# Attention's probabilities turned in 32x32 blocks and moved by ScalarE's DMA queue, in a two-block layer stack

## The chip, the cores and the metric

One core of one Trainium2 chip. The metric is the device time of one execution in microseconds, of which three were taken. The profile is of one execution of its own.

## The reference

Two stacks of two layers each, on 256 tokens of width 2048, in float32. The first (a hybrid of windowed attention, spatial gating and gated linear attention) is the same before and after. The change lies in the second:

```python
h = x @ w_in                       # q, k, v, z for 12 heads "a" and 12 heads "b", 128 wide; forget and gate logits
qa, ka = rope(qa), rope(ka)
out_a = dilated_mixture(qa, ka, va)              # causal softmax attention, banded patterns
out_b = softmax(qb @ kb.T * 128**-0.5 + cum[t] - cum[s], causal) @ vb
up_a, up_b = (out_a * silu(za)) @ w_up_a, (out_b * silu(zb)) @ w_up_b
y = (g_a * up_a + g_b * up_b) @ w_out
x = layer_norm(alpha * x + y)
```

The kernel computes out_a as one softmax over all 256 keys, with the logarithm of how often a key occurs in the patterns added to its score (mask_a).

## The kernel before, in words

**Stream of granules.** The weights of a layer come as granules of 256 rows by 512 columns (512 KB), into a ring of four slots (`raw`). SyncE loads them (L310) when VectorE has done with a slot. ScalarE copies a granule to `whi` rounded to the float32r format (`hi`, L372) once TensorE has given back the slot that is four granules older. VectorE subtracts to get the rest, `wlo` (`lo`, L489). TensorE multiplies high by high, low by high and high by low: twelve matmuls of 512 columns a granule (`accumulate`, L860), of which the last four wait for `wlo`. Eight granules are one chunk of 512 output columns. The plan of chunks (`second_plan`) is q, k, v, z for each group of four heads, three groups, then four gate chunks, four up-projections, the same once more for heads "b", then four output chunks. There are six groups a layer and two layers, so twelve groups in all.

**Attention is written into this stream by hand.** For each group r counts granules from the start of its q chunk (`group_step`), and each engine does its part of the attention at fixed r, behind its work on the granule (ScalarE, VectorE) or ahead of it (TensorE: `fills2` into the two banks psT, `units2` into the two banks psS). Since ScalarE and VectorE work ahead of TensorE, step r is not the same moment on all engines.

- r = 12 to 14 and 20 to 22: q and k are rotated (VectorE, heads "a") or copied (ScalarE, heads "b") into `stage`. Then VectorE turns 32x32 blocks (L615) from `stage` into `blocks`, and POOL issues 16 DMAs (L325), which move each quarter of the partitions to each quarter of the columns. This makes qT and kT, features on partitions. A DMA moves 32 partitions with eight pieces of 128 bytes.
- r = 26, 27, 28: score units s0 (four heads, tokens 0 to 127), s1 and s2 (two heads each, tokens 128 to 255, 256 keys), L829. An f32 matmul is two passes, each with a weight load of its own.
- r = 30, 31, 32: VectorE adds the mask or bias and takes the row maxima (L642 to L648). r = 31, 32, 33: ScalarE takes the exponentials with their row sums (L416); at r = 31 it also copies v out.
- r = 31, 32, 33 on TensorE: the 128x128 probabilities are transposed against an identity, four per unit (L812, into psT). r = 35, 36, 37: ScalarE copies them to `probT` (L392).
- r = 36, 37: output units o0 and o1 (L839), with `probT` as the stationary operand and v moving.
- r = 38: ScalarE evacuates z with Silu (L429). r = 39: reciprocals. r = 40, 41: VectorE scales and multiplies by z (L664, L668). r = 42: VectorE turns the blocks of the product into `zb` (L674), and POOL issues 16 DMAs to zT, which shares memory with `probT`. r = 50: ScalarE and VectorE split zT into `ahi` and `alo` for the up-projection (L437, L731).

POOL issues its DMAs in the order q, k, z of each group (`regrouped`), with the gate rows between. SyncE's queue has only the weights and the result.

In the first block, L2147 on VectorE multiplies `zt` in place by a transposed operand, both read as pieces of m elements with a gap of m elements, for m = 128, 64, 32, 16, 8, 4, 2 and 1:

```python
a = zt[:, i % 2, :].rearrange("p (n s m) -> p n s m", s=2, m=m)[:, :, half, :]
last = dve.tensor_tensor(a, a, b, ALU.mult)
```

## Time and profile before

| | |
|---|---|
| runs (median, lowest to highest of 3) | 2801.91 us, 2800.36 to 2802.63 us |
| profiled execution, its own time | 2799.75 us |
| its span, first to last instruction | 2798.0 us |
| mean granted TensorE clock | 0.994 of full speed |
| instructions | 35964 |
| DMA | 622.74 MB, 223 GB/s |

The profile lists the work of each engine, PE for TensorE's matmuls and PEld for its weight loads, DVE for VectorE, ACT for ScalarE, POOL for GpSimd and SPq for SyncE's DMA issues. L860 is line 860 of the kernel. Durations of single matmuls overlap, so that of a stretch is read from the starts. The first block takes the first 839 us or so; the second the rest.

### The profile page before, as it was taken

The page shows a single profiled execution, that of the slowest core. Times are in us where ns is not written, and L with a number is a line of the kernel's source. Part 1 is how long each engine was busy: PE and PEld are TensorE (multiplying, and loading weights), DVE is VectorE, ACT ScalarE, POOL GpSimd, SP SyncE. Part 2 cuts the span into 40 slices and gives each one's busy share as a digit, 9 for nine tenths or more (in the row PEclk, how much of TensorE's full clock was granted, in tenths as well). Part 3 has the DMA queues.
Part 4 walks back from the last instruction along what each step waited for, and adds up shares of the span by engine and source line. Part 5 has one row for each costly group of instructions (what it writes and reads, how often), then busy time and mean ns, then how long its engine had stood idle before and what let it go on. Part 6 is the DMA issues. An engine that isn't in the chain of part 4 may idle for free.

```text
span 2798.0 us, 35964 instructions
## 1 busy us (share of the span) xinstructions
PE 2757.6 (99%) x13157; PEld 2253.2 (81%) x13157; DVE 1817.0 (65%) x2220; ACT 1346.3 (48%) x1765; POOL 370.9 (13%) x653
## 2 busy tenths in 40 slices
PE   8899999999999999999999999999999999999998
PEld 5477887888888888888888888888888888888886
DVE  7889899778657556655555556575565545555565
ACT  3255646556544453544444544444445444445443
POOL 0000010000001223100133100022131011331000
PEclk9999999999999999999999999999999999999999
DMA  9987798865655566566566566565566665665554
GB/s 397 414 311 241 272 342 307 309 222 190 215 194 181 188 201 205 185 220 196 191 202 203 191 196 223 181 195 187 191 203 205 208 199 183 206 206 187 193 213 148
DMA packets 178617, 622.74 MB, mean 223 GB/s; under 512 B 27688, under 2 KB 27984, under 8 KB 173088
## 3 DMA queue, kind: packets, MB, share of 16 engines
q1 hardware_dynamic: 155376, 583.08, 60.3%
q0 software_dynamic: 23088, 37.56, 4.6%
q8 instruction: 104, 1.70, 0.3%
q14 instruction: 49, 0.40, 0.0%
HBM read 599.51 MB, written 2.14 MB: 215 GB/s over the span
## 4 chain that ended last, share of the span: by engine, by line
PE 90%; DMA 4%; DVE 4%; ACT 1%; issue 0%; SPq 0%; DVEq 0%; ACTq 0%
PE acc L860 65%; PE acc L2455 16%; DMA raw<-in_w 2%; DVE wlo L1865 1%; PE psS L839 1%; PE psS L829 1%; DMA scr<-in_w_early 1%; PE psS L2455 1%; PE psS L2421 1%; PE psT L812 1%; PE psT L2378 1%; DMA mraw<-in_w_early 1%; DVE raw L1900 0%; PE psS L2440 0%; PE psT L2340 0%
## 5 line engine op out<-in xcount | busy, mean ns | idle before, releaser
L489 DVE TENSOR_TENSOR wlo<-raw,whi 128x1024 fp32r<-128x1024 f32 x670 | 819.4, 1224 | 783.7 <-ACT whi L372 782.0
L372 ACT ACTIVATE whi<-raw 128x1024 fp32r<-128x1024 f32 x670 | 708.9, 1059 | 980.3 <-PE acc L860 964.4
L860 PE MATMUL acc<-whi,tokens_hi 128*128 128x512 f32 x2304 | 632.3, 395 | 0.5 <-DVE tokens_lo L303 0.3
L860 PE MATMUL acc<-whi,tokens_lo 128*128 128x512 f32 x2304 | 618.2, 389 | 0.0
L860 PE MATMUL acc<-wlo,tokens_hi 128*128 128x512 f32 x2304 | 618.1, 389 | 0.0
L860 PEld LDWEIGHTS acc<-whi,tokens_lo 128*128 128x128 f32 x2304 | 432.4, 188 | 91.5
L860 PEld LDWEIGHTS acc<-wlo,tokens_hi 128*128 128x128 f32 x2304 | 432.4, 188 | 91.0
L860 PEld LDWEIGHTS acc<-whi,tokens_hi 128*128 128x128 f32 x2304 | 425.7, 188 | 85.6 <-DVE tokens_lo L303 0.9
L1564 ACT ACTIVATE whi<-raw 128x1024 fp32r<-128x1024 f32 x160 | 168.7, 1058 | 200.8 <-PE acc L2455 116.2
L1865 DVE TENSOR_TENSOR wlo<-raw,whi 128x1024 fp32r<-128x1024 f32 x160 | 195.3, 1223 | 82.2 <-ACT whi L1564 81.3
L2455 PE MATMUL acc<-whi,tokens_hi 128*128 128x512 f32 x800 | 226.1, 403 | 1.9 <-DVE tokens_lo L1974 1.2
L2455 PE MATMUL acc<-wlo,tokens_hi 128*128 128x512 f32 x800 | 215.6, 390 | 0.7 <-DVE wlo L1865 0.7
L2455 PE MATMUL acc<-whi,tokens_lo 128*128 128x512 f32 x800 | 215.6, 390 | 0.0
L325 POOL DMA_DIRECT2D probT<-prob x192 | 110.3, 583 | 619.4 <-DVE prob L674 619.4
L2455 PEld LDWEIGHTS acc<-wlo,tokens_hi 128*128 128x128 f32 x800 | 150.0, 188 | 33.3 <-DVE wlo L1865 1.4
L2455 PEld LDWEIGHTS acc<-whi,tokens_lo 128*128 128x128 f32 x800 | 150.2, 188 | 32.8
L2455 PEld LDWEIGHTS acc<-whi,tokens_hi 128*128 128x128 f32 x800 | 143.0, 188 | 35.3 <-issue 3.5
L325 POOL DMA_DIRECT2D qT<-blocks x192 | 110.5, 584 | 448.6 <-DVE blocks L615 447.6
L325 POOL DMA_DIRECT2D kT<-blocks x192 | 110.2, 583 | 149.3 <-DVE blocks L615 149.3
L860 PE MATMUL acc<-whi,ahi 128*128 128x512 f32 x384 | 103.2, 391 | 0.0
L1564 ACT ACTIVATE whi<-mraw 128x1024 fp32r<-128x1024 f32 x64 | 67.7, 1058 | 73.2 <-PE acc L2455 59.7
L860 PE MATMUL acc<-wlo,ahi 128*128 128x512 f32 x384 | 102.7, 389 | 0.0
(355 smaller groups left out, 2434.2 us busy)
## 6 DMA issues: line engine op xcount, KB each, us to landing
raw<-in_w SPq DMA_DIRECT2D x838, 512.0 KB, 4.2
raw<-in_w_late SPq DMA_DIRECT2D x80, 512.0 KB, 5.0
mraw<-in_w SPq DMA_DIRECT2D x64, 512.0 KB, 4.7
mraw<-in_w_late SPq DMA_DIRECT2D x48, 512.0 KB, 4.8
y<-in_w_early SPq DMA_DIRECT2D x12, 1024.0 KB, 15.4
mraw<-in_w_early SPq DMA_DIRECT2D x7, 1024.0 KB, 14.9
scr<-in_w_early SPq DMA_DIRECT2D x7, 1024.0 KB, 14.8
sgl<-in_w_early SPq DMA_DIRECT2D x6, 1024.0 KB, 15.0
```

What stands on the lines that cost most here:

```text
L325: pool.dma_start(dst[c * QUAD:(c + 1) * QUAD, :, b * QUAD:(b + 1) * QUAD], src[b * QUAD:(b + 1) * QUAD, :, c * QUAD:(c + 1) * QUAD]).then_ ...
L372: act.activation(whi[:, n % SLOTS, :], raw[:, n % SLOTS, :], ACT.Copy).then_inc(s_hi, 1)
L489: dve.tensor_tensor(wlo[:, n % SLOTS, :], raw[:, n % SLOTS, :], whi[:, n % SLOTS, :].bitcast(F32), ALU.subtract).then_inc(s_lo, 1)
L812: t = pe.transpose(bank[:, k * P:(k + 1) * P], prob[:, name[2], k * P:(k + 1) * P], ident[:])
L829: m = pe.matmul(out, qT[:, h, tb * P:(tb + 1) * P], kT[:, h, 0:w], start=True, stop=True)
L839: m = pe.matmul(bank[:, h * HD:(h + 1) * HD], probT[:, u, col * P:(col + 1) * P], v[:, s, h * HD:(h + 1) * HD], start=(s == 0), stop=(s == ...
L860: m = pe.matmul(acc[c % 2][:, tb, :], a[:, kk, tb * P:(tb + 1) * P], b[:, n % SLOTS, k * CW:(k + 1) * CW], start=(kk == 0 and q == 0), sto ...
L1564: act.activation(whi[:, n % SLOTS, :], slot(("w", n)), ACT.Copy).then_inc(s_hi, 1)
L1865: dve.tensor_tensor(wlo[:, n % SLOTS, :], slot(("w", n)), whi[:, n % SLOTS, :].bitcast(F32), ALU.subtract).then_inc(s_lo, 1)
L2378: t = pe.transpose(bank[:, k * SEQ + tb * P:k * SEQ + (tb + 1) * P], src[:, tb, cols[k]:cols[k] + P], ident[:])
L2421: m = pe.matmul(out[:, k * P:(k + 1) * P], key[rows, kcol:kcol + P], query[rows, qcol:qcol + P], start=True, stop=True)
L2455: m = pe.matmul(bank_a(gc)[:, tb, :], a[:, kt, tb * P:(tb + 1) * P], b[:, n % SLOTS, k * CW:(k + 1) * CW], start=(g == 0 and k == 0 and q ...
```

## The change

- **Probabilities.** TensorE's twelve identity transposes a group and ScalarE's three copies go. At r = 33 (R_PROB) VectorE waits for all exponentials and turns the blocks of all 1536 columns in one instruction, into `pb`, which lies over qT and half of kT (now one tile `qkT`). At r = 34 ScalarE waits for that, and for the previous group's `alo`, and issues 16 DMAs on its own queue to `pT` (all of `probT`). Each moves 32 partitions with one piece of 1536 bytes.
- **Long pieces.** VectorE writes turned blocks so that what one DMA moves lies together: q, k and z go in one piece of 1 KB a partition. For this q and the probabilities are laid out `by_column` (a token's 8, or 12, values side by side), k and z `by_quad` (runs of 32). TensorE reads qT with a step of 8 elements and pT with a step of 12 as stationary operands, and kT as moving operand in runs of 32. z is kept in the order of heads (`zheads`).
- **Order.** All three score units stand at r = 26, s2 in a psT bank. Both output units stand at r = 37. VectorE takes the scores at r = 29 to 31, ScalarE the exponentials at r = 30 to 32. VectorE's outputs move to r = 41 and 42, z's blocks to 43. `s_blk` counts four per group instead of three. POOL's q and k moves wait for the previous group's probabilities (`s_pT`) instead of its scores, and its z move no longer waits for `alo`.

The other lines of the diff only renumber waits (3 to 4 per group, `16 * QUADS * QUADS` to `MOVED`).

```diff
--- before.py
+++ after.py
@@ -83,10 +83,12 @@

 R_Q, R_K = 14, 22
 R_SCORES = 26
-R_BLOCKS = R_SCORES + 16
+R_PROB = R_SCORES + 7
+R_BLOCKS = R_SCORES + 17
 R_SPLIT = 50
 QUAD = 32
 QUADS = P // QUAD
+MOVED = 16 * QUADS * QUADS
...
@@ -109,8 +111,8 @@
     if c == 0:
         out += [("x", 0), ("x", 1)] if g == 0 else [("x", g + 1)] if g < KT // 2 - 1 else []
     for grp, r in group_step(c, g):
-        if 0 <= r - R_SCORES - 5 <= 2:
-            out += [("p", grp, r - R_SCORES - 5)]
+        if r == R_SCORES:
+            out += [("s", grp, 2)]
     if c and CHUNKS2[c - 1][0] == "u" and CHUNKS2[c - 1][1] >= NCW and g == 3:
         j = CHUNKS2[c - 1][1] - NCW
...
@@ -121,10 +123,10 @@

     out = []
     for grp, r in group_step(c, g):
-        if 0 <= r - R_SCORES <= 2:
-            out += [("s", grp, r - R_SCORES)]
-        if 0 <= r - R_SCORES - 10 <= 1:
-            out += [("o", grp, r - R_SCORES - 10)]
+        if r == R_SCORES:
+            out += [("s", grp, 0), ("s", grp, 1)]
+        if r == R_SCORES + 11:
+            out += [("o", grp, 0), ("o", grp, 1)]
...
     alo = sb("alo", [P, KT_UP, SEQ], F32R)
     gb = sb("gb", [P, TB, D])
     stage = sb("stage", [P, TB, CW])
-    qT = sb("qT", [P, HPG, SEQ])
-    kT = sb("kT", [P, HPG, SEQ])
+    qkT = sb("qkT", [P, 2 * HPG, SEQ])
+    qT, kT = qkT[:, 0:HPG, :], qkT[:, HPG:, :]
     v = sb("v", [P, TB, CW])
     z = sb("z", [P, TB, CW])
     prob = sb("prob", [P, 3, CW])
     probT = sb("probT", [P, 3, CW])
-    zb = prob[:, 0:TB, :].rearrange("p b (k t) -> p (b k) t", t=HD)
-    zT = probT[:, 0:TB, :].rearrange("p b (k t) -> p (b k) t", t=HD)
+    pT = probT[:].rearrange("p u n -> p (u n)")
+    pb = qkT[:].rearrange("p h t -> p (h t)")[:, 0:3 * CW]
+    zb = prob[:, 0:TB, :].rearrange("p b t -> p (b t)")
+    zT = probT[:, 0:TB, :].rearrange("p b t -> p (b t)")
     blocks = sb("blocks", [P, TB, CW])
     rtmp = blocks[:, 1, :]
-    heads = stage[:].rearrange("p b n -> p (b n)").rearrange("p (h b e) -> p b h e", b=TB, e=HD)
+    heads, zheads = (t[:].rearrange("p b n -> p (b n)").rearrange("p (h b e) -> p b h e", b=TB, e=HD)
+                     for t in (stage, z))
     mask_a = sb("mask_a", [P, P + SEQ])
...
         return psT[FILL2[name] % 2]

+    def by_feature(tile):
+
+        return tile.rearrange("p (k c j) -> p k c j", c=QUADS, j=QUAD)
+
+    def by_quad(tile):
+
+        return tile.rearrange("p (c k j) -> p k c j", c=QUADS, j=QUAD)
+
+    def by_column(tile):
+
+        return tile.rearrange("p (c j k) -> p k c j", c=QUADS, j=QUAD)
+
     def attended_views(grp):

         k = HPG * (grp % 3)
-        return [t[:, k:k + HPG, :].rearrange("p k (b t) -> p b k t", b=TB) for t in (ahi, alo)] + [
-            zT.rearrange("p (b k) t -> p b k t", b=TB)]
+        return [by_feature(t[:, k:k + HPG, :].rearrange("p k t -> p (k t)")) for t in (ahi, alo)] + [by_quad(zT)]
...

+    def blocks_moved(queue, dst, src, signal):
+
+        dst, src = (t.rearrange("p (c n) -> p c n", c=QUADS) for t in (dst, src))
+        for b in range(QUADS):
+            for c in range(QUADS):
+                queue.dma_start(dst[c * QUAD:(c + 1) * QUAD, b, :], src[b * QUAD:(b + 1) * QUAD, c, :])\
+                    .then_inc(signal, 16)
+
     def gpsimd(pool):
         pool.wait_ge(s_ym, NCW * DEPTH)
         for tile, name in ((mask_a, "mask_a"), (mask_b, "mask_b"), (tables, "tables")):
             pool.dma_start(tile[:], dram[name]).then_inc(s_const, 16)
-        def blocks_moved(dst, src, signal):
-
-            for b in range(QUADS):
-                for c in range(QUADS):
-                    pool.dma_start(dst[c * QUAD:(c + 1) * QUAD, :, b * QUAD:(b + 1) * QUAD],
-                                   src[b * QUAD:(b + 1) * QUAD, :, c * QUAD:(c + 1) * QUAD]).then_inc(signal, 16)
-
         def regrouped(l, grp):

             n = NGRP * l + grp
             for i, (dst, signal) in enumerate(((qT, s_qT), (kT, s_kT))):
-                pool.wait_ge(s_blk, 3 * n + i + 1)
-                if grp:
-                    pool.wait_ge(*unit_full(l, ("s", grp - 1, 2)))
-                elif l:
-                    pool.wait_ge(*unit_full(l - 1, ("s", NGRP - 1, 2)))
-                blocks_moved(dst[:].rearrange("p h (b t) -> p (h b) t", b=TB),
-                             blocks[:].rearrange("p b (k t) -> p (b k) t", t=HD), signal)
-            pool.wait_ge(s_blk, 3 * n + 3)
-            if n:
-                pool.wait_ge(s_alo, n)
-            blocks_moved(zT, zb, s_zT)
+                pool.wait_ge(s_blk, 4 * n + i + 1)
+                if n:
+                    pool.wait_ge(s_pT, MOVED * n)
+                blocks_moved(pool, dst.rearrange("p h t -> p (h t)"), blocks[:].rearrange("p b t -> p (b t)"), signal)
+            pool.wait_ge(s_blk, 4 * n + 4)
+            blocks_moved(pool, zT, zb, s_zT)
...
-            def fill_copy(name, dst):
-                act.wait_ge(*filled(l, name))
-                act.activation(dst, bank_t(name)[:], ACT.Copy).then_inc(s_tfree[FILL2[name] % 2], 1)
-
             def evacuate(c, dst, func, scale=1.0):
                 act.wait_ge(*multiplied(l, c))
                 src = acc[c % 2][:]
-                if dst is heads:
+                if dst is not v:
                     src = src.rearrange("p b (h e) -> p b h e", e=HD)
...
@@ -418,18 +427,19 @@
                     p.then_inc(s_exp, 1)
                 if r == 31:
                     evacuate(c0 + 2, v, ACT.Copy)
-                if 0 <= r - R_SCORES - 9 <= 2:
-                    u = r - R_SCORES - 9
-                    if u == 0 and NGRP * l + grp:
-                        act.wait_ge(s_alo, NGRP * l + grp)
-                    fill_copy(("p", grp, u), probT[:, u, :])
+                if r == R_PROB + 1:
+                    n = NGRP * l + grp
+                    act.wait_ge(s_blk, 4 * n + 3)
+                    if n:
+                        act.wait_ge(s_alo, n)
+                    blocks_moved(act, pT, pb, s_pT)
                 if r == R_SCORES + 12:
                     if NGRP * l + grp:
-                        act.wait_ge(s_blk, 3 * (NGRP * l + grp))
-                    evacuate(c0 + 3, z, ACT.Silu)
+                        act.wait_ge(s_blk, 4 * (NGRP * l + grp))
+                    evacuate(c0 + 3, zheads, ACT.Silu)
...
                     dve.wait_ge(*acc_read(l, group_chunk(grp) + which))
                 if which:
-                    dve.wait_ge(s_qT, 16 * QUADS * QUADS * (NGRP * l + grp + 1))
-                dve.transpose(blocks[:].rearrange("p b n -> p (b n)"), stage[:].rearrange("p b n -> p (b n)"))\
+                    dve.wait_ge(s_qT, MOVED * (NGRP * l + grp + 1))
+                dve.transpose((by_column, by_quad)[which](blocks[:].rearrange("p b n -> p (b n)")),
+                              by_feature(stage[:].rearrange("p b n -> p (b n)")))\
                     .then_inc(s_blk, 1)

...
-                if 0 <= r - R_SCORES - 4 <= 2:
-
-                    u = r - R_SCORES - 4
+                if 0 <= r - R_SCORES - 3 <= 2:
+
+                    u = r - R_SCORES - 3
                     name = ("s", grp, u)
-                    bank = UNIT2[name] % 2
+                    if u < 2:
+                        bank, full, free = psS[UNIT2[name] % 2], unit_full(l, name), s_sfree[UNIT2[name] % 2]
+                        read = unit_read(l, name)
+                    else:
+                        bank, full, free = bank_t(name), filled(l, name), s_tfree[FILL2[name] % 2]
+                        read = copied(l, name)
...
-                    dve.wait_ge(*unit_full(l, name))
+                    dve.wait_ge(*full)
...
-                    dve.tensor_tensor(p, psS[bank][:].rearrange("p (h s) -> p h s", s=w), m, ALU.add)\
-                        .then_inc(s_sfree[bank], 1)
-                    dve.wait_ge(*unit_read(l, name))
+                    dve.tensor_tensor(p, bank[:].rearrange("p (h s) -> p h s", s=w), m, ALU.add).then_inc(free, 1)
+                    dve.wait_ge(*read)
...
+                if r == R_PROB:
+                    dve.wait_ge(s_exp, at(l, 3 * NGRP, 3 * grp + 3))
+                    dve.transpose(by_column(pb), by_feature(prob[:].rearrange("p u n -> p (u n)"))).then_inc(s_blk, 1)
...
-                if 0 <= r - R_SCORES - 14 <= 1:
-
-                    tb = r - R_SCORES - 14
+                if 0 <= r - R_SCORES - 15 <= 1:
+
+                    tb = r - R_SCORES - 15
                     name = ("o", grp, tb)
                     bank = UNIT2[name] % 2
                     dve.wait_ge(*unit_full(l, name))
...
-                    dve.tensor_tensor(z[:, tb, :], z[:, tb, :], rtmp, ALU.mult).then_inc(s_att, 1)
+                    dve.tensor_tensor(zheads[:, tb], zheads[:, tb], t, ALU.mult).then_inc(s_att, 1)
                 if r == R_BLOCKS:
                     n = NGRP * l + grp
                     dve.wait_ge(s_att, TB * (n + 1))
-                    if n:
-                        dve.wait_ge(s_zT, 16 * QUADS * QUADS * n)
-                    dve.transpose(zb.rearrange("p a t -> p (a t)"), z[:].rearrange("p b n -> p (b n)")).then_inc(s_blk, 1)
+                    dve.wait_ge(s_blk, 4 * n + 3)
+                    dve.transpose(by_quad(zb), by_feature(z[:].rearrange("p b n -> p (b n)"))).then_inc(s_blk, 1)

...
+            def turned_heads(tile):
+
+                return tile.rearrange("p h t -> p (h t)").rearrange("p (c h t j) -> p h t c j", c=QUADS, h=HPG, t=TB)
+
+            def queries(tile):
+
+                return tile.rearrange("p h t -> p (h t)").rearrange("p (t h b) -> p h b t", h=HPG, b=TB)
+
+            def scores(name, bank):
+
+                _, grp, u = name
+                pe.wait_ge(s_qT, MOVED * (NGRP * l + grp + 1))
+                pe.wait_ge(s_kT, MOVED * (NGRP * l + grp + 1))
+                w, tb = (P, 0) if u == 0 else (SEQ, 1)
+                for b in range(CW // w):
+                    h = b + max(0, 2 * (u - 1))
+                    m = pe.matmul(bank[:, b * w:(b + 1) * w].rearrange("p (t c j) -> p t c j", c=QUADS, j=QUAD),
+                                  queries(qT)[:, h, tb], turned_heads(kT)[:, h, 0:tb + 1], start=True, stop=True)
+                return m
...
                 else:
-
-                    pe.wait_ge(s_exp, at(l, 3 * NGRP, 3 * name[1] + name[2] + 1))
-                    for k in range(4):
-                        t = pe.transpose(bank[:, k * P:(k + 1) * P], prob[:, name[2], k * P:(k + 1) * P], ident[:])
+                    t = scores(name, bank)
...
                 if name[0] == "s":
-                    _, grp, u = name
-                    if u == 0:
-                        pe.wait_ge(s_qT, 16 * QUADS * QUADS * (NGRP * l + grp + 1))
-                        pe.wait_ge(s_kT, 16 * QUADS * QUADS * (NGRP * l + grp + 1))
-                    w, tb = (P, 0) if u == 0 else (SEQ, 1)
-                    for b in range(CW // w):
-                        h = b + max(0, 2 * (u - 1))
-                        out = bank[:, b * w:(b + 1) * w]
-                        m = pe.matmul(out, qT[:, h, tb * P:(tb + 1) * P], kT[:, h, 0:w], start=True, stop=True)
+                    m = scores(name, bank)
...
                     _, grp, tb = name
                     if tb == 0:
                         pe.wait_ge(*acc_read(l, group_chunk(grp) + 2))
-                    for p in ((0,), (1, 2))[tb]:
-                        pe.wait_ge(*copied(l, ("p", grp, p)))
+                        pe.wait_ge(s_pT, MOVED * (NGRP * l + grp + 1))
                     for h in range(HPG):
                         for s in range(tb + 1):
                             u, col = (0, h) if tb == 0 else (1 + h // 2, 2 * (h % 2) + s)
-                            m = pe.matmul(bank[:, h * HD:(h + 1) * HD], probT[:, u, col * P:(col + 1) * P],
+                            m = pe.matmul(bank[:, h * HD:(h + 1) * HD], pT.rearrange("p (t k) -> p k t", k=3 * HPG)[:, HPG * u + col],
                                           v[:, s, h * HD:(h + 1) * HD], start=(s == 0), stop=(s == tb))
```

## Rows read from the trace of the kernel before

**Rows 1.** The page, first part: span, busy time, share and instructions

```profile
span 2798.0 us, 35964 instructions
...
PE 2757.6 (99%) x13157; PEld 2253.2 (81%) x13157; DVE 1817.0 (65%) x2220; ACT 1346.3 (48%) x1765; POOL 370.9 (13%) x653
```

**Rows 2.** Waits of PE, 850 to 2780 us: total, times, longest

```profile
PE psT L802 <- DVE x L525: 0.9, 1, 0.9
PE acc L860 <- DVE tokens_lo L495: 0.2, 1, 0.2
```

**Rows 3.** Waits of all engines, whole span: total us, times, longest

```profile
ACT whi L372 <- PE acc L860: 964.4, 577, 5.5
DVE wlo L489 <- ACT whi L372: 782.0, 582, 4.4
...
ACT whi L372 <- DMA raw<-in_w: 15.8, 9, 4.6
```

**Rows 4.** Chain that ended last, 900 to 1030 us: start, us, what

```profile
921.88 0.89 PE psS L829 x8
922.78 2.74 PE acc L860 x12
925.51 0.86 PE psS L829 x4
...
930.01 8.21 PE acc L860 x36
938.22 0.44 PE psT L812 x4
938.66 2.77 PE acc L860 x12
...
945.07 8.21 PE acc L860 x36
953.28 0.89 PE psS L839 x8
...
956.90 1.78 PE psS L839 x16
958.69 57.14 PE acc L860 x252
```

**Rows 5.** Groups by shape, PE, from 640 us: busy us, mean ns

```profile
L812 PE MATMUL psT<-ident,prob 128*128 128x128 f32 x144 | 21.5, 271 | 0.0
```

**Rows 6.** Timeline of ACT, 920 to 985 us: start, us, instruction, idle before

```profile
921.98 1.06 ACT L372 ACTIVATE whi<-raw 128x1024 fp32r<-128x1024 f32 x1 [1.66 <-PE acc L860]
...
930.32 1.28 ACT L416 ACT_TABLE_LOAD   x1
...
942.50 0.58 ACT L392 ACTIVATE probT<-psT 128x512 f32<-128x512 f32 x1
```

**Rows 7.** Timeline of DVE, 918 to 985 us

```profile
926.70 1.23 DVE L489 TENSOR_TENSOR wlo<-raw,whi 128x1024 fp32r<-128x1024 f32 x1 [2.40 <-ACT whi L372]
...
966.48 1.24 DVE L674 STREAM_TRANSPOSE prob<-z 128x1024 f32<-128x1024 f32 x1
```

**Rows 8.** Line L2147, DVE: ns min/median/max, first and last start

```profile
L2147 DVE TENSOR_TENSOR zt<-zt,gain x32: 415/417/420, 191.2 to 669.2; 128x256 f32<-128x256 f32 x32
```

**Rows 9.** SyncE's issues: line L310, and the timeline, 28.0 to 29.2 us

```profile
L310 SPq DMA_DIRECT2D raw<-in_w x668: 332/333/353, 839.2 to 2766.3; - x167
...
28.10 0.33 SPq L1461 DMA_DIRECT2D y<-in_w_early  x1
28.47 0.43 SPq L1467 DMA_DIRECT2D b_kT<-in_w  x1
```

**Rows 10.** POOL's issues: timeline 907 to 925 us, and line L325

```profile
907.64 9.18 POOL L325 DMA_DIRECT2D kT<-blocks  x16 [12.17 <-DVE blocks L615]
...
L325 POOL DMA_DIRECT2D kT<-blocks x192: 582/582/593, 907.6 to 2512.7; - x192
...
DMA to landing us min/median/max: 1.8/3.0/5.4
```

More of the change, by code:

```diff
@@ L216, in second_block @@
     s_kT = sem("c_kT")
+    s_pT = sem("c_pT")
     s_zT = sem("c_zT")
@@ L403, in attention @@
                 if grp >= 3 and r == R_Q - 2:
-                    act.wait_ge(s_blk, 3 * (NGRP * l + grp) - 1)
+                    act.wait_ge(s_blk, 4 * (NGRP * l + grp) - 2)
                     evacuate(c0, heads, ACT.Copy, SCALE2)
                 if grp >= 3 and r == R_K - 2:
-                    act.wait_ge(s_blk, 3 * (NGRP * l + grp) + 1)
+                    act.wait_ge(s_blk, 4 * (NGRP * l + grp) + 1)
                     evacuate(c0 + 1, heads, ACT.Copy)
-                if 0 <= r - R_SCORES - 5 <= 2:
-                    u = r - R_SCORES - 5
+                if 0 <= r - R_SCORES - 4 <= 2:
+                    u = r - R_SCORES - 4
                     act.wait_ge(s_max, at(l, 3 * NGRP, 3 * grp + u + 1))
@@ L420, in attention @@
                     evacuate(c0 + 2, v, ACT.Copy)
[L421 to L425 removed]
+                if r == R_PROB + 1:
[4 more added lines that the diff above has]
+                    blocks_moved(act, pT, pb, s_pT)
                 if r == R_SCORES + 12:
                     if NGRP * l + grp:
[L428 to L429 removed]
+                        act.wait_ge(s_blk, 4 * (NGRP * l + grp))
+                    evacuate(c0 + 3, zheads, ACT.Silu)
                 if r == R_SPLIT:
                     hi_view, _, src = attended_views(grp)
[L432 removed]
+                    act.wait_ge(s_zT, MOVED * (NGRP * l + grp + 1))
                     if grp >= 3:
@@ L582, in rope @@
                     if which:
-                        dve.wait_ge(s_blk, 3 * n + 1)
-                        dve.wait_ge(s_qT, 16 * QUADS * QUADS * (n + 1))
+                        dve.wait_ge(s_blk, 4 * n + 1)
+                        dve.wait_ge(s_qT, MOVED * (n + 1))
                     elif n:
-                        dve.wait_ge(s_blk, 3 * n - 1)
+                        dve.wait_ge(s_blk, 4 * n - 2)
                 half = HD // 2
@@ L637, in attention @@
                             dve.wait_ge(s_cmask, l + 1)
-                    dve.wait_ge(*unit_full(l, name))
+                    dve.wait_ge(*full)
                     if u == 0 and NGRP * l + grp:
-                        dve.wait_ge(s_zT, 16 * QUADS * QUADS * (NGRP * l + grp))
+                        dve.wait_ge(s_zT, MOVED * (NGRP * l + grp))
                     p = prob[:, u, :].rearrange("p (h s) -> p h s", s=w)
-                    dve.tensor_tensor(p, psS[bank][:].rearrange("p (h s) -> p h s", s=w), m, ALU.add)\
-                        .then_inc(s_sfree[bank], 1)
-                    dve.wait_ge(*unit_read(l, name))
+                    dve.tensor_tensor(p, bank[:].rearrange("p (h s) -> p h s", s=w), m, ALU.add).then_inc(free, 1)
+                    dve.wait_ge(*read)
                     if grp >= 3 and u == 0:
@@ L659, in attention @@
                         dve.wait_ge(*acc_read(l, c0 + 3))
-                        dve.wait_ge(s_kT, 16 * QUADS * QUADS * (NGRP * l + grp + 1))
+                        dve.wait_ge(s_kT, MOVED * (NGRP * l + grp + 1))
                     else:
```

1 line of the change is left out of this document (removed).

## The prediction

> **What bounds the kernel now.** Four views, in this order. The page's first part: TensorE is busy for 99% of the span, VectorE and ScalarE for 65% and 48% [rows 1]. A busy share of pipelined matmuls could still hide waiting, so next the waits, asked over the second block: TensorE has two, together 1.1 us, both at a layer's start [rows 2], while ScalarE waits 964 us for TensorE (it splits a granule as soon as TensorE has given a ring slot back) and VectorE 782 us for ScalarE [rows 3]. So in the second block the time is that of TensorE's own queue. Third, the chain of waits around one group of heads, which in this stretch is TensorE alone [rows 4]. Outside attention 252 matmuls take 57.14 us: 0.2268 us each, 2.72 us a granule of twelve. The attention work stands between the granules as extra pieces. A second group, a layer later, has the same pieces within 0.01 us, so one group is read and taken twelve times (2 layers of 6). Fourth, the timelines of ScalarE and VectorE around that group [rows 6, 7], because the change hands work to both, and an engine that is not the bound becomes it once a granule comes late.
>
> **Removed from TensorE.** 144 transposes [rows 5], twelve a group, in three pieces of 0.44 us, and a granule beside such a piece is drawn at 2.76 to 2.77 or (three of them) 8.21 instead of 2.72 and 8.16: 3 x 0.44 + 3 x 0.05 = 1.47 us a group [rows 4]. Twelve groups: 17.6 us. Nothing else hides this work, so all of it is on the path.
>
> **Merged on TensorE.** The three score units now stand together, and so do the two output units. Each break between kinds of matmul costs some 0.02 to 0.05 us (0.89, 0.86, 0.86 and granules of 2.74, 2.77 and 8.21 in place of 2.72 and 8.16). Two breaks of scores and one of outputs go: about 0.1 us a group, 1.2 us in all.
>
> **The operands' layout, the open price.** The number of attention matmuls and columns stays. But the stationary operand of the scores (queries) is now read with 8 elements, 32 bytes, from one column to the next, and that of the outputs (probabilities) with 12, 48 bytes; before both were contiguous. The keys, which move, come in runs of 32 elements. No row shows TensorE reading a spread operand. The lower bound is nothing: the nearest row of any spread read is VectorE's multiplication in the first block, whose pieces shrink from 128 elements to one with a gap as long, and all 32 of them take 415 to 420 ns [rows 8]. It reaches only a step of 8 bytes, on another engine. The upper bound: a load that takes two steps a column. A pass of 128 columns has a pitch of 0.89/8 = 0.111 us, where load and pass are about equally long, and a pass of 256 columns 0.86/4 = 0.215 us [rows 4] (an f32 product is two passes, so s0 has 8, each later score unit 4, the outputs 8 and 16). If a spread load lasts as long as the 256-column pass, the 8 + 24 short passes rise from 0.111 to 0.215: 3.3 us a group, 40 us in all; the 256-column ones cover it. A gain from the layout is excluded: passes and columns are the same. I take nothing, since the one measured row says so, and keep 40 us for the range and for a rival.
> The Trainium skill speaks against the change here: "Advanced Engine Details and Errata", section "SBUF Cachelines", says memory is read in lines of 16 bytes, needs at least two hits on a line to hide the access, and pays when every access is in another line. Eight or twelve f32 elements apart is another line each time. The multiplication of [rows 8], with two elements a line, doesn't contradict it. By it the sum would end near the upper bound, at 2821, which is the result of the first rival.
>
> **ScalarE.** Three copies of 0.58 us a group go; it waits for TensorE there [rows 3, 6], so they are worth nothing. What it gains: 16 DMA issues at granule step 34 with two waits in front, on the previous group's low half (done at step 18, long past) and on VectorE's turned blocks. No row shows ScalarE issuing a DMA. Bounds: SyncE's issues take 0.33 us, one straight behind another 0.43 us, starts 0.37 us apart [rows 9]; POOL's take 0.58 us [rows 10], which is descriptor work of another kind. Nearest is SyncE's: I take 0.40, 6.4 us for the sixteen, with 5.3 and 9.3 us as ends. Queued behind them is the split of granule 35, for which TensorE waits. Let T be TensorE's start of granule 31, when slot and step 34 of ScalarE come free (each split starts as a granule ends: 921.98 with the first score at 921.88 [rows 4, 6]). The split of 34 lasts until T+1.1 (1.06 us). VectorE at step 33: the previous splits end at about T-1.1 by ScalarE's timeline moved one step forward [rows 6] (split, table load 1.28, four exponentials, v's evacuation, two more pairs), its subtraction costs 1.14 from start to start, so the new transpose runs from T+0.1. It is 1536 elements wide against 1024 at 1.24 us [rows 7]: 1.86 us, until T+1.95. ScalarE idles 0.85 us there. Issues until T+8.35, split of 35 until T+9.4. TensorE starts granule 35 at T + 4 x 2.72 = T+10.9. Slack 1.5 us, and afterwards ScalarE catches up, 1.06 us against 2.72. The point from which TensorE waits is an issue of 0.49 us. Cost taken: nothing, covered by the four-slot ring.
>
> **VectorE.** 12 transposes of 1.86 us, 22 us in all, and the same additions and maxima one step earlier. In the second block it mostly waits for ScalarE [rows 3]; granule 33 costs it 1.2 + 1.9 us against 2.72, and its lead over TensorE is several us (it subtracts granule 30 at 926.70 [rows 7]; TensorE comes to it after 935, two granules of 2.72 behind 930.01 [rows 4]). Nothing. If the blocks' spread output slowed it to double, only ScalarE's wait would grow, by 1.9 us.
>
> **POOL and the moves.** POOL issues as many DMAs as before (192 three times, 0.58 us each), with pieces of 1 KB where there were eight of 128 bytes. Keys: last issue at 916.8, landing 3.0 us (up to 5.4) after an issue, scores at 921.88 [rows 4, 10]: same distance as before, about 2 us. The turned z comes one granule later (step 43), is issued over 9.2 us and is wanted at step 50, 19 us on; the next queries may wait about 1 us behind it and have the 22 us until the keys. The probabilities' transfers are 16 x 48 KB, at most 6.4 + 4 us after T+1.95, and the outputs stand at granule 37, T+16.3: covered by 4 us. SyncE's loads share the DMA engines, but ScalarE waited only 15.8 us on them in all [rows 3], and the slot of 35 freed 5 us late still leaves its next load landed before TensorE needs it.
>
> **Sum.** Profiled execution: 2799.75 us (span 2798.0, 1.75 outside) [rows 1]. 2799.75 - 17.6 - 1.2 = 2781.0. The median of the runs is 2801.9, 2.2 above the profiled one, so I forecast 2782. About 0.2%, 5.6 us, is what a measurement here can tell from no change.
>
> **Rivals.**
> 1. *Spread weight loads become the bound* (chance 0.36, slower). Place: the eight passes of s0 and the 24 of the outputs. Price +40 us, so 2821 to 2823. It decides against the change from 0.16 us a load instead of 0.111: 18.8/(12 x 32) = 0.05 us more cancels the gain. For: these passes have load and pass equally long, so nothing hides a longer load. Against: the even 415 to 420 ns of [rows 8].
> 2. *ScalarE's issues hold up the split of granule 35* (0.10). At POOL's 0.58 us the issues end at T+11.2, the split at T+12.3: 1.4 us waiting a group, 17 us; result 2782 to 2799, and still below before unless VectorE's transpose is slow as well (another 1.9 us a group, 22 us).
> 3. *Both* (0.10): 2828 to 2862.
> 4. *A load dearer by about half the bound* (0.06): 2797 to 2807, no change.
> That the change doesn't do what it says, that is, the transposes leave TensorE and nothing falls, would need a wait that TensorE doesn't have before [rows 2]; it is in rivals 2 and 3.
>
> **Numbers.** The forecast's own case has 0.38, 2778 to 2785. Faster by over 0.2% (below 2796.3): 0.38 and most of rival 2, 0.46. Within: part of rivals 2 and 4, 0.10. Slower: rivals 1 and 3 and the rest, 0.44. The range goes from 2778 up over rival 1 with a little waiting, to 2829; most of rival 3 is left out.
>
> **What the profile will show.** No identity transposes of probabilities; TensorE's chain with one piece of scores of 16 passes and one of outputs of 24. Right: those take 2.6 and 2.7 us, so 5.3 together. Rival 1: outputs near 5.1 us and s0 near 1.7, weight loads of these lines longer than 188 ns or with gaps of 0.2 us. Rival 2: waits of TensorE on ScalarE's whi, twelve times, near granule 35. ScalarE's issues at 0.33 to 0.43 us would confirm the slack; the wide transpose at 1.86 us VectorE's term. The forecast is wrong if any pass of 128 columns has a pitch above 0.16 us or if TensorE waits over 1.5 us a group.

## The result and the profile after

The changed kernel takes 2915.6 us (median of 4 runs, 2911.1 to 2916.7), against 2801.5 for the kernel before: a ratio of 1.0405 (95% interval 1.0393 to 1.0418), 114 us slower. The prediction was 2782, with 2829 as the upper end.

The page's first part, to be held against [rows 1]:

```profile
span 2913.1 us, 35810 instructions
...
PE 2822.9 (97%) x13013; PEld 2315.8 (79%) x13013; DVE 1858.4 (64%) x2232; ACT 1324.8 (45%) x1729; POOL 321.3 (11%) x653
```

The 144 transposes are gone, yet TensorE is busy for 65 us more, and its span has grown by 115: there is slower work and there is idle time. The waits of TensorE, 850 to 2900 us, name the idle time; before there were only waits of the last two kinds, 1.1 us in all ([rows 2]):

```profile
PE acc L885 <- ACT whi L385: 48.7, 12, 4.9
PE psT L839 <- DVE x L535: 1.1, 2, 0.9
PE acc L885 <- DVE tokens_lo L505: 0.2, 1, 0.2
```

Twelve waits, one a group, for ScalarE's split of a granule. The chain of waits of the first group says what stands behind it (start, us, what; compare [rows 4]):

```profile
921.00 0.94 PE psT L816 x4
921.95 2.87 PE psS L816 x12
924.82 2.78 PE acc L885 x12
...
938.78 2.92 DVE qkT L666
941.71 0.60 ACTq L339
...
952.36 1.06 ACT whi L385
...
953.47 7.36 PE acc L885 x24
960.83 6.30 PE psS L864 x24
967.12 57.17 PE acc L885 x252
```

VectorE's wide transpose ends at 941.7, ScalarE's queue then issues sixteen transfers until 952.3, the next split comes at 952.36, and TensorE starts granule 35 at 953.47. ScalarE's timeline shows the burst as one line:

```profile
941.71 10.54 ACTq L339 DMA_DIRECT2D probT<-qkT  x16
952.36 3.90 ACT L385 ACTIVATE whi<-raw 128x1024 fp32r<-128x1024 f32 x4 [12.74 <-issue]
```

Two more things are in the chain. The scores take 0.94 + 2.87 = 3.81 us, the outputs 6.30, where before they took 2.61 and 2.67. And the two granules behind the wait take 7.36 us where 5.44 are due. The table by stretches (us, PE, PEld, DVE, ACT, POOL busy, then the granted TensorE clock, DMA share, GB/s) shows why:

```profile
942.00:948.30 6.30, 6.30 (x30) 5.21 (x29) 0.73 (x1) 0.00 (x0) 0.00 (x0) 1.00 0.51 147
949.00:953.47 4.47, 0.34 (x3) 0.01 (x1) 0.03 (x1) 1.11 (x2) 0.00 (x0) 1.00 0.29 77
953.47:957.92 4.45, 4.45 (x12) 3.49 (x13) 4.45 (x4) 4.42 (x5) 0.00 (x0) 0.62 0.39 131
957.92:960.66 2.74, 2.74 (x13) 2.30 (x12) 1.25 (x2) 1.62 (x2) 0.00 (x0) 1.00 0.97 298
```

After the idle stretch the granted clock is 0.62 of full speed on average, a mixture of the levels 1.2 and 2.4 GHz, and the twelve matmuls of that granule take 4.45 us for 2.72. One granule later it is full again. Not every group is like the first. In the second the wait is 4.9 us, and the granule behind it looks like this:

```profile
1057.50:1062.79 5.29, 5.29 (x12) 4.13 (x13) 4.62 (x4) 5.10 (x5) 0.00 (x0) 0.50 0.54 153
```

It takes 5.29 us, all of it at the lower level. Summed over the twelve groups (from the starts of the matmuls), the two granules behind the wait take 90.8 us where 65.3 are due: 26 us more, and not twelve times the first group's 1.7. The single lines (ns min/median/max) show the slow loads, and VectorE's writing:

```profile
L864 PEld LDWEIGHTS psS<-v,probT x288: 342/369/373, 960.4 to 2670.6; 128*128 128x128 f32 x144
L816 PEld LDWEIGHTS psS<-qkT x144: 335/336/338, 921.6 to 2628.6; 128*128 128x128 f32 x144
...
L625 DVE STREAM_TRANSPOSE blocks<-stage x24: 1239/1686/2169, 883.7 to 2608.7; 128x1024 f32<-128x1024 f32 x24
L666 DVE STREAM_TRANSPOSE qkT<-prob x12: 2972/2977/2989, 938.7 to 2643.1; 128x1536 f32<-128x1536 f32 x12
...
L339 ACTq DMA_DIRECT2D probT<-qkT x192: 514/612/1382, 941.7 to 2656.0; - x192
L339 POOL DMA_DIRECT2D probT<-prob x192: 496/496/546, 979.2 to 2692.9; - x192
```

**Theory A**, as it stood before the experiments: three losses per group. The spread operands cost (3.81 - 2.61) + (6.30 - 2.67) = 4.8 us, the wait 4.1, the low clock behind it 1.7. Twelve times: 58 + 49 + 21 = 128 us, less the 18.8 that the prediction counted as gain, is 109 of the 114. The 21 are the first group's 1.7 us taken twelve times; with the 26 us of all twelve in their place the sum is 114. The rivals, one against each term: the wait comes from VectorE and not from the queue (B); the passes are slow by the moving keys or by contention with the transfers (D, E); the clock is low for another reason (M).

### The profile page after: what moved, and what is told of

Its sections match the earlier page's. It is cut to its first block, busy times and chain, and to the rows that moved or that the text cites. A ratio compares the mean times of both kernels' runs of the same rounds, so it can differ in the third digit from the quotient of the medians.

```text
span 2913.1 us, 35810 instructions
## 1 busy us (share of the span) xinstructions
PE 2822.9 (97%) x13013; PEld 2315.8 (79%) x13013; DVE 1858.4 (64%) x2232; ACT 1324.8 (45%) x1729; POOL 321.3 (11%) x653
## 4 chain that ended last, share of the span: by engine, by line
PE 79%; DVE 6%; ACT 5%; DMA 4%; ACTq 4%; issue 1%; SPq 0%; DVEq 0%
PE acc L885 55%; PE acc L2480 15%; ACTq L339 4%; DMA raw<-in_w 3%; PE psS L864 3%; ACT whi L385 2%; ACT prob L425 1%; DVE wlo L1890 1%; DVE qkT L666 1%; PE psS L816 1%; DMA scr<-in_w_early 1%; PE psS L2480 1%; PE psS L2446 1%; DMA mraw<-in_w_early 1%; ACT L425 1%
## 5 line engine op out<-in xcount | busy, mean ns | idle before, releaser
L885 PE MATMUL acc<-whi,tokens_hi 128*128 128x512 f32 x2304 | 635.1, 397 | 49.3 <-ACT whi L385 48.7
L885 PE MATMUL acc<-whi,tokens_lo 128*128 128x512 f32 x2304 | 627.3, 394 | 0.0
L885 PEld LDWEIGHTS acc<-whi,tokens_hi 128*128 128x128 f32 x2304 | 435.3, 191 | 144.4 <-ACT whi L385 53.8
L885 PEld LDWEIGHTS acc<-whi,tokens_lo 128*128 128x128 f32 x2304 | 439.2, 191 | 93.5
L339 POOL DMA_DIRECT2D qkT<-blocks x384 | 187.7, 497 | 606.0 <-DVE blocks L625 603.0
L2480 PE MATMUL acc<-whi,tokens_lo 128*128 128x512 f32 x800 | 215.6, 390 | 0.0
L339 POOL DMA_DIRECT2D probT<-prob x192 | 93.9, 497 | 791.8 <-DVE prob L691 520.3
L2480 PEld LDWEIGHTS acc<-whi,tokens_lo 128*128 128x128 f32 x800 | 150.2, 188 | 32.8
L2480 PEld LDWEIGHTS acc<-whi,tokens_hi 128*128 128x128 f32 x800 | 143.0, 188 | 35.3 <-issue 3.7
L885 PE MATMUL acc<-whi,alo 128*128 128x512 f32 x384 | 102.6, 389 | 0.0
```

The source lines that it names most:

```text
L339: queue.dma_start(dst[c * QUAD:(c + 1) * QUAD, b, :], src[b * QUAD:(b + 1) * QUAD, c, :])\
L885: m = pe.matmul(acc[c % 2][:, tb, :], a[:, kk, tb * P:(tb + 1) * P], b[:, n % SLOTS, k * CW:(k + 1) * CW], start=(kk == 0 and q == 0), sto ...
L2480: m = pe.matmul(bank_a(gc)[:, tb, :], a[:, kt, tb * P:(tb + 1) * P], b[:, n % SLOTS, k * CW:(k + 1) * CW], start=(g == 0 and k == 0 and q ...
```

## The experiments

Each kernel was run beside the kernel before, on the same chip.

**e1: only the queue is changed,** ScalarE's for POOL's, where the transfers stand between the moves of k and z.

```diff
-                if r == R_PROB + 1:
...
-                    blocks_moved(act, pT, pb, s_pT)
+            pool.wait_ge(s_blk, 4 * n + 3)
+            if n:
+                pool.wait_ge(s_alo, n)
+            blocks_moved(pool, pT, pb, s_pT)
```

> The changed kernel, with one part undone: the 16 transfers of the probabilities are issued by POOL (behind the keys' move, ahead of z's) instead of by ScalarE. Theory A, three terms: per group 4.13 us in which TensorE waits for the split of granule 35, 1.73 us more for the granule after it at a granted clock of 0.62, and 4.8 us of slower attention passes. By A the first two go: 2915.6 - 12 x 5.86 = 2845, TensorE's waits on whi at zero, clock near 1.00 all along, passes unchanged (scores 3.8 us, outputs 6.2 us a group). Rival B, the wait comes from VectorE's slow transpose (2.98 us instead of 1.86) and not from the queue: the wait stays in part, 2880 or more. Rival C, POOL's sixteen issues land too late for the outputs at granule 37: TensorE waits at L864 instead, over 2860.

Measured: 2853.5 us, ratio 1.0183 (1.0166 to 1.0200). TensorE doesn't wait for a split any more, and no granule runs at a low clock. What it waits for, and how its outputs run (waits, then the chain):

```profile
PE psS L862 <- DMA probT<-qkT: 7.4, 11, 1.1
```

```profile
958.59 6.66 PE psS L862 x24
```

So the queue carries the wait (B falls: VectorE's transpose still takes 2.99 us here). Rival C is right on a small scale: POOL's transfers land up to 1.1 us late at the outputs. Those 7.4 us are most of the 8.5 between the 2845 expected and the result; behind such a wait the outputs also take 6.66 us for 6.30. The clock does still fall in three of the twelve groups (mean 0.992 for 0.994), but during the outputs. The outputs of the first group and of the third:

```profile
958.59:965.02 6.43, 6.43 (x25) 6.43 (x25) 1.29 (x2) 0.84 (x1) 0.00 (x0) 1.00 0.52 168
1154.56:1160.99 6.43, 6.43 (x25) 6.43 (x25) 1.23 (x1) 0.37 (x1) 0.00 (x0) 0.74 0.52 172
```

The same 24 passes take the same time at either granted clock, so these three falls cost nothing: what the outputs last is set by the slow loads.

**e2: only TensorE's reading is changed.**

```diff
-                                  queries(qT)[:, h, tb], turned_heads(kT)[:, h, 0:tb + 1], start=True, stop=True)
+                                  qT[:, h, tb * P:(tb + 1) * P], turned_heads(kT)[:, h, 0:tb + 1], start=True, stop=True)
...
-    pT.rearrange("p (t k) -> p k t", k=3 * HPG)[:, HPG * u + col]
+    pT[:, (HPG * u + col) * P:(HPG * u + col + 1) * P]
```

> The changed kernel, but TensorE reads its stationary operands (queries, probabilities) as 128 neighbouring columns instead of with a step of 8 and 12; everything else stays, VectorE's spread writing and ScalarE's queue too. Part changed: the scores and outputs are formed from the wrong columns. Theory A: passes of 128 columns return to 0.111 us (scores 2.6 us, outputs 2.7 us a group), so 2915.6 - 12 x 4.8 = 2858, while ScalarE's wait and the low clock after it stay. Rival D, the slow passes come from the keys as moving operand in runs of 32: the scores stay at 3.8 us, only the outputs fall, 2872. Rival E, the slow passes are contention with the transfers: nothing falls, 2910 to 2915.

Measured: 2861.9 us, ratio 1.0221 (1.0204 to 1.0238). The chain:

```profile
924.30 0.86 PE psT L816 x4
925.16 1.76 PE psS L816 x12
...
955.59 7.39 PE acc L885 x24
962.98 2.68 PE psS L864 x24
```

Both kinds of pass are back at 0.11 us, with the keys still moving in runs of 32 and the transfers as before: D and E fall. The wait (48.4 us) and the slow pair of granules (7.39) stay, as A says; so it doesn't take slow passes to bring the low clock. The 4 us above A's 2858 go with the clock as well: the four runs had mean granted clocks of 0.980 to 0.984, the lower the longer, and the one at 0.984 took 2858.1 us.

**e3 and e4: a contiguous layout that computes the right thing.** The turned blocks are written in runs of 32, and short pieces, as in the kernel before, put the runs of a head side by side, so that a stationary operand is 128 neighbouring columns with the right values:

```diff
+    def short_moved(queue, dst, src, signal):
+        dst = dst.rearrange("p (k t) -> p k t", t=P)
+        src = src.rearrange("p (c k j) -> p c k j", c=QUADS, j=QUAD)
...
+                queue.dma_start(dst[c * QUAD:(c + 1) * QUAD, :, b * QUAD:(b + 1) * QUAD],
+                                src[b * QUAD:(b + 1) * QUAD, c]).then_inc(signal, 16)
...
-                    dve.transpose(by_column(pb), by_feature(prob[:].rearrange("p u n -> p (u n)"))).then_inc(s_blk, 1)
+                    dve.transpose(by_quad(pb), by_feature(prob[:].rearrange("p u n -> p (u n)"))).then_inc(s_blk, 1)
-                    blocks_moved(act, pT, pb, s_pT)
+                    short_moved(act, pT, pb, s_pT)
```

with q likewise, and the operands read as in e2. That is e3; in e4 POOL issues the probabilities' transfers, as in e1.

> The changed kernel with queries and probabilities laid out as before, in runs of 32 that the DMA puts side by side (pieces of 128 bytes, 12 a partition for the probabilities), so that stationary operands are contiguous and VectorE's writing is too; keys and z stay in long pieces, ScalarE's queue stays. Theory A: no slow passes (-58 us), VectorE's wide transpose at 1.86 us instead of 2.98, so the split of granule 35 comes 1.1 us sooner: TensorE's wait falls from 4.1 to 3.0 us a group and the low clock after it may stay: 2915.6 - 58 - 13 = 2845 (2820 if the clock stays up). Rival F, short pieces make ScalarE's issues dearer than 0.64 us: 2860 or more.

Measured: 2842.8 us, ratio 1.0148 (1.0131 to 1.0165). VectorE's wide transpose is down to 1.77 us, and the wait shrinks by only 0.6 us a group. Waits, then ScalarE's timeline:

```profile
PE acc L894 <- ACT whi L394: 41.1, 12, 4.6
```

```profile
940.87 10.83 ACTq L348 DMA_DIRECT2D probT<-qkT  x16
```

The transpose ends 1.2 us sooner, but the burst lasts 0.3 us longer (F, in small). In ten of the twelve groups the granule behind the wait runs at a low clock. In the other two the clock stays full after waits of 3.1 and 3.2 us, and the two granules take 5.6 us for 5.44, so some 0.15 us a group is the restart and not the clock. Waits as short were followed by a low clock elsewhere in this run; what decides it is not shown.

> As e3, with POOL issuing the probabilities' transfers as well: what is left of the change is the removal of the transposes and the merged units. Theory A: all three losses gone, so the gain that the prediction counted is there: 2801.5 - 17.6 - 1.2 = 2783, TensorE without waits, scores 2.6 us and outputs 2.7 us a group. Rival G, something else in the change costs time (the order with all scores in one place, z a granule later, DMA load): 2790 or more, with a wait of TensorE that the trace names.

Measured: 2791.8 us, ratio 0.9967 (0.9955 to 0.9980): now faster than before. What it lacks from 2783 is in one line of the waits:

```profile
PE psS L871 <- DMA probT<-qkT: 8.6, 10, 1.6
```

Behind that wait the outputs take a little longer than before's 2.67 us (chain):

```profile
955.18 2.92 PE psS L871 x24
```

POOL takes 0.62 us an issue for twelve short pieces, and its transfers land 4.1 us after the issue (ScalarE's: 2.1), so the last is late for the outputs. Rival G, if only as this wait.

**e5 and e6: the price of a load by its step.** e1 with other steps. The diff is that of e5; e6 has 3 in place of 2 and 6 in place of 4:

```diff
-    queries(qT)[:, h, tb]
+    qT.rearrange("p h t -> p (h t)")[:, min(SEQ * h + P * tb, 2 * CW - 2 * P):][:, 0:2 * P].rearrange("p (t k) -> p t k", k=2)[:, :, 0]
-    pT.rearrange("p (t k) -> p k t", k=3 * HPG)[:, HPG * u + col]
+    pT[:, min(P * (HPG * u + col), 3 * CW - 4 * P):][:, 0:4 * P].rearrange("p (t k) -> p t k", k=4)[:, :, 0]
```

> e1 (POOL issues the transfers), with TensorE reading the queries with a step of 2 elements (8 bytes) and the probabilities with a step of 4 (16 bytes). Part changed: scores and outputs are formed from the wrong columns. Theory A2, the load pays for every new 16-byte line (the Trainium skill, "Advanced Engine Details and Errata", section "SBUF Cachelines"): step 2 costs nothing (scores 2.6 us a group, e2), step 4 costs as much as step 8 or more (outputs 24 x 0.24 = 5.8 us). Rival H, the price grows with the step all the way: step 4 clearly below step 8, outputs 3.5 to 4.5 us, and step 12 then dearer than step 8 for the same reason (0.262 against 0.239 us).

> As e5 with a step of 3 (12 bytes) for the queries and 6 (24 bytes) for the probabilities. Part changed: scores and outputs are formed from the wrong columns. By A2 step 3, with 1.33 elements a line, lies between: 0.11 to 0.24 us a pass, scores 2.6 to 3.8 us; step 6 is as dear as step 8: outputs 5.8 us. By rival H step 6 lies between the values of 4 and 8.

Measured, one run each: 2829.5 and 2831.7 us. The chain of e5, then that of e6 (s0 and s1 are the x12 piece, the outputs x24):

```profile
923.52 1.80 PE psS L814 x12
956.17 5.84 PE psS L862 x24
```

```profile
923.40 2.25 PE psS L814 x12
955.85 5.61 PE psS L862 x24
```

In both runs the outputs stand behind a wait for POOL's transfers, as in e1, so the two x24 pieces are some 0.25 us too long for their passes. The price is therefore taken inside each stretch, as the median time from the start of one 128-column pass to the start of the next (steps 1, 8 and 12 from e9 and e7):

| step, elements | 1 | 2 | 3 | 4 | 6 | 8 | 12 |
|---|---|---|---|---|---|---|---|
| bytes | 4 | 8 | 12 | 16 | 24 | 32 | 48 |
| us a pass | 0.112 | 0.118 | 0.173 | 0.233 | 0.224 | 0.239 | 0.267 |

Nearly free at step 2, and 0.22 to 0.27 us from step 4 on, where every column lies in another 16 bytes. 32, 64, 96 and 128 pieces of 16 bytes are touched at steps 1 to 4, and from step 2 to step 4 a pass costs 1.8 ns for each of them. Step 6 is cheaper than step 4, so H falls; the 0.03 to 0.04 us by which step 12 is dearer than 4 and 6 are not explained by lines. This agrees with the Trainium skill ("Advanced Engine Details and Errata", section "SBUF Cachelines": at least two hits on a line, or a penalty), here with 0.233 against 0.112 us as the penalty. Only f32 was run, so nothing here tells 16 bytes from four elements.

**e8: is ScalarE's issue dear by its shape?**

```diff
-                    blocks_moved(act, pT, pb, s_pT)
+                    for i in range(QUADS * QUADS):
+                        act.dma_start(pT[:, 96 * i:96 * (i + 1)], pb[:, 96 * i:96 * (i + 1)]).then_inc(s_pT, 16)
```

> The changed kernel with ScalarE's 16 transfers in another shape: all 128 partitions with 96 columns each, the same 48 KB, from and to the same columns. Part changed: the blocks are not regrouped, so the outputs are formed from the wrong elements. Theory K, an issue of a DMA that covers 32 of 128 partitions is dear by its shape: it falls from 0.61 us to SyncE's 0.33 to 0.43, the sixteen take 5 to 7 us, the split of granule 35 is ready before TensorE comes, and TensorE's 49 us of waiting and the low clock after it are gone (2845). Rival L, it is ScalarE's queue (an issue straight behind an issue): it stays at 0.61 and so does everything else, 2910.

Measured: 2915.9 us, an issue still 0.62 us at the median, the wait still 49.3 us. K falls; L was not yet shown.

**e9: the sixteen shared by two queues.** e4, with blocks b = 0, 1 issued by ScalarE at step 34 and b = 2, 3 by POOL, with a semaphore each.

> e4 (contiguous operands) with the probabilities' sixteen transfers shared, eight issued by ScalarE and eight by POOL. Theory A: ScalarE is held for 8 x 0.64 = 5.1 us, the split of granule 35 ends at T+8.2 before TensorE's T+10.9; the last transfer lands about T+11, before the outputs at T+16.3, so the 8.7 us that TensorE waited for transfers in e4 go: 2801.1 - 18.8 = 2782, ratio 0.993. Rival G: another loss stays, 2788 or more.

Measured: 2779.2 us, ratio 0.9931 (0.9917 to 0.9944). This beats both kernels. TensorE has no wait in the second block but the short ones at a layer's start, 1.3 us in all, and its chain is its own again:

```profile
920.05 0.86 PE psT L831 x4
920.91 1.76 PE psS L831 x12
922.67 29.93 PE acc L901 x132
952.60 2.68 PE psS L880 x24
...
1012.41 0.86 PE psT L831 x4
```

From one group's scores to the next it is 92.36 us; before it was 958.69 + 57.14 - 921.88 = 93.95 ([rows 4]). The 1.59 us a group are 19.1 in all, where the prediction's sum had 18.8.

**e7: the same sharing with everything else of the change left in.**

> The changed kernel with its spread operands, long pieces and slow transpose, but with the probabilities' sixteen transfers shared: eight issued by ScalarE, eight by POOL. Theory A: ScalarE is held for about 5.1 us from the end of VectorE's 2.98 us transpose, the split of granule 35 ends near T+9.4, before TensorE's T+10.9, so the wait (49 us) and with it the low clock of the next granule (21 us) go: 2845, passes as slow as before (outputs 6.3 us). Rival M, the low clock comes from the slow passes or from elsewhere and not from the wait: the granted clock stays low somewhere in each group, 2860 or more.

Measured: 2840.1 us, ratio 1.0144 (1.0127 to 1.0160). ScalarE's timeline and the stretches around the outputs:

```profile
942.33 5.11 ACTq L340 DMA_DIRECT2D probT<-qkT  x8
947.54 3.91 ACT L391 ACTIVATE whi<-raw 128x1024 fp32r<-128x1024 f32 x4 [7.31 <-PE acc L892]
```

```profile
947.00:955.00 8.00, 8.00 (x37) 6.60 (x36) 4.87 (x5) 7.16 (x7) 0.00 (x0) 1.00 0.71 190
955.40:961.70 6.30, 6.30 (x25) 6.30 (x25) 1.93 (x3) 1.06 (x1) 0.00 (x0) 1.00 0.84 303
```

No wait, no low clock, and the slow outputs run at a full clock: M falls as it stood, since slow passes alone don't lower the clock. A 4 us wait does so without them (e2). With short waits it took the slow passes too: the clock fell during the slow outputs in three groups of e1, one of e5 and two of e6, whose waits were at most 1.1 us, and in none of e4 and e11, whose operands are contiguous and whose waits go up to 2.1 us.

**e11: the sixteen on ScalarE's queue in two bursts,** b = 0, 1 at step 34 and b = 2, 3 at step 36, contiguous operands.

> e3 (contiguous operands, all sixteen transfers on ScalarE's queue) with the issues in two bursts: eight at granule step 34, eight at step 36. Theory A: what costs is the length of one burst against the ring's slack, not ScalarE's queue as such: the splits of 35 and 36 get through between the bursts, TensorE doesn't wait for them; the last transfer lands about T+16.4 where the outputs stand at T+16.3, so up to 1 us a group may be waited there: 2782 to 2794. Rival L2, ScalarE's queue is too slow in any cut: TensorE waits as in e3, 2830 or more.

Measured: 2797.3 us, ratio 0.9991 (0.9981 to 1.0000), 3 us above what A gave. The waits have moved from the split to the outputs:

```profile
PE psS L875 <- DMA probT<-qkT: 14.0, 12, 2.1
```

So ScalarE's queue can carry all sixteen without holding up a split; L2 falls. The transfers then land 1.2 us a group too late, more than the 1 us that A allowed.

**e10: the price of an issue by itself,** behind the end of e9, where nothing else runs.

```diff
+        for src in (flat[:, 0:384], dram["w"][0][:, 0:384]):
+            for b in range(QUADS):
+                for c in range(QUADS):
+                    queue.dma_start(flat[c * QUAD:(c + 1) * QUAD, 1024 + 384 * b:1408 + 384 * b],
+                                    src[b * QUAD:(b + 1) * QUAD]).then_inc(signal, 16)
```

> e9 with a measurement behind its end, where nothing else runs: SyncE issues 16 transfers inside the on-chip memory (32 partitions, 1536 bytes each) and 16 of the same shape from HBM, then ScalarE the same 32, then ScalarE eight more with a copy of its own before each. Added: only these transfers, so the total time is not to be compared. Theory L, issues in a burst on ScalarE's queue are dear by themselves: ScalarE 0.6 us each here too, SyncE 0.33 to 0.43, and the eight spaced ones nearer 0.33. Rival N, the price is that of a burst of any queue, or of transfers inside the memory: SyncE's sixteen take 0.6 us too. Rival O, the price comes from the other traffic in the kernel (loads of SyncE at the same time): here both take 0.33 to 0.43.

Measured, on SyncE's timeline and then on ScalarE's:

```profile
2780.55 10.09 SPq L333 DMA_DIRECT2D raw<-raw  x16
2791.97 7.54 SPq L333 DMA_DIRECT2D raw<-in_w  x16
```

```profile
2801.02 10.18 ACTq L333 DMA_DIRECT2D raw<-raw  x16
2812.53 7.48 ACTq L333 DMA_DIRECT2D raw<-in_w  x16
...
2822.08 0.53 ACTq L521 DMA_DIRECT2D raw<-raw  x1
```

N is right, and L falls: the two queues are alike, 0.63 us an issue from on-chip memory to on-chip memory in a burst (from start to start; the issue itself 0.59 to 0.61) and 0.47 from HBM in the same shape. When ScalarE does something between, the issue itself takes 0.51 to 0.53. O falls too, since the price is there without other traffic.

## Why the prediction was wrong

**The forecast's own case** was that spread loads cost nothing and the ring covers ScalarE's burst. Neither held, and it was the case of *both*, rival 3, given a chance of 0.10 and 2828 to 2862, that came, 54 us above even its upper end.

- *Removed and merged work* was right: 18.8 us forecast, 19.1 by e9's pitch of the groups, 21.3 by its total.
- *The operands' layout* is the first step that failed: "I take nothing, since the one measured row says so". The row of VectorE's multiplication has two elements in every 16 bytes, and e5 shows that TensorE, too, reads that step almost for free. It was no evidence for a step of 32 bytes. The upper bound of 40 us was also too low, since it let a load last as long as a 256-column pass, 0.215 us, and left those passes out. Measured were 0.24 us a pass in s0 and 0.26 in the outputs, on average, and 0.08 us more per later score unit: 4.8 us a group, 58 in all. The difference of e7 and e9 says 61.
- *ScalarE's issue* is the second: "Nearest is SyncE's: I take 0.40". The row was of loads from HBM over all 128 partitions, and the transfers are a burst inside the on-chip memory; by e8 and e10 it is the source that makes most of the difference, and not the 32 partitions (0.62 us with 128) or the queue. The term was 6.4 us and measured 10.5; even the upper end, POOL's 9.3, was too low. The turning point of 0.49 us an issue, from which TensorE waits, was in the text and was passed.
- *VectorE's transpose* was taken by its width, 1.86 us. Contiguous it is 1.77, but written with a step of 12 it takes 2.98. The prediction named "another 1.9 us" as a possible delay, and 1.1 of it came. With 10.5 us for the burst and 2.98 for the transpose the prediction's own working gives T+0.1+2.9+10.5+1.1 = T+14.6 against T+10.9: a wait of 3.7 us, where 4.1 was measured. The working held, its prices didn't.
- *The clock* was missing. The text priced a wait of TensorE at its own length. After 4.1 us of waiting the next granule ran at 0.62 of the full clock and took 1.7 us more; over the twelve groups it was 26 us, some 2 of them the restart. In e4, after 0.8 us, the outputs took 2.92 us for 2.68, with a granted clock of 1.00.

The sum from the runs: after minus e7 is 75 us (wait 49, slow granules behind it 26), e7 minus e9 is 61 (spread loads, where the passes give 58), e9 minus before is -21. That these differences add up to the 114 measured, to within 1 us, is no evidence, since each starts where the last ends; the evidence is that each one agrees with what its trace shows.

The Trainium skill says ("DMA: Bandwidth & Descriptors", section "Issuing engines are not separate DMA queues") that another issuing engine only saves the time of initiating a DMA, usually small beside the transfer. For a single transfer the trace agrees, 0.61 us to issue it and 2.0 us from issue to landing. But the landings overlap and the issues do not: the sixteen took 10.5 us of ScalarE's time, and that saving was what decided here.

## What to carry to other kernels

Before a layout is changed so that a transfer's pieces become long, look at who reads the result: a stationary f32 operand with a step of four elements or more doubled its pass here, and short pieces cost 0.1 us of POOL an issue. A burst of DMA issues belongs to the engine whose time nobody waits for. If it must sit in front of work that is awaited, its length is to be held against the ring's slack, and split over two queues when it is too long. Price an issue from a row of the same kind of transfer, and a wait of TensorE of several us with the slow granules behind it (here half as much again: 26 us behind 49).

## What the runs showed of the hardware

- A pass of 128 f32 columns by the step of its stationary operand: 0.11 us at step 1, 0.12 at 2, 0.17 at 3, 0.22 to 0.27 from 4 to 12 elements (e9, e5, e6, e7).
- Such slow passes last as long at a granted clock of 0.74 as at 1.00 (e1), whereas a granule of twelve matmuls takes 5.29 us at 0.50 for 2.72 at 1.00 (the changed kernel).
- VectorE's 32x32 transpose of 128x1024 f32 takes 1.24 us written in runs of 32, and 2.17 with a step of 8; of 128x1536 it takes 1.77 and, with a step of 12, 2.98.
- Issues in a burst, from start to start: 0.63 us inside the memory and 0.47 from HBM, on SyncE and ScalarE alike. POOL's: 0.50 us with one piece a partition, 0.58 with eight and 0.62 with twelve.
- The keys as moving operand in runs of 32 cost nothing (e2).
- TensorE's clock fell behind waits of 3.1 to 5.0 us in all but two of the 48 groups of four runs (the changed kernel, e2, e3, e8), and never behind waits of up to 2.1 us with contiguous operands (e4, e11).
